# Gated recurrence: the multiplier taken from tanh and a squared, with the order of ScalarE's exponentials, roots and gelus changed

## The reference, cut to what matters

```
def rglru_block(h, w_in, conv_w, conv_b, w_a, b_a, w_x, b_x, lam, w_o):
    proj = h @ w_in
    gate = jax.nn.gelu(proj[..., :RG_WIDTH])
    xc = causal_depthwise_conv_2(proj[..., RG_WIDTH:], conv_w, conv_b)
    ...
    r = jax.nn.sigmoid(... + b_a);  i = jax.nn.sigmoid(... + b_x)
    log_a = (-RG_C * r) * jax.nn.softplus(-lam)
    a = jnp.exp(log_a)
    mult = jnp.sqrt(-jnp.expm1(2.0 * log_a))
    bterm = mult * (i * xc)
    _, hs = lax.associative_scan(lru_combine, (a, bterm), axis=1)
    return (hs * gate) @ w_o
```

## Time and profile before

| what | value |
|---|---|
| median of 3 runs | 1074.45 us (1071.22 to 1075.06) |
| the profiled execution | 1074.95 us, of which the span is 1072.9 us |
| mean granted TensorE clock | 0.992 |
| PE busy | 1022.1 us, 95% of the span |
| DVE busy | 690.9 us, 64% |
| ACT busy | 614.2 us, 57% |

### The profile page before, as it was taken

One profiled execution on the slowest core, in us unless ns is written; L12 is line 12 of the kernel. 1 busy time (PEld: TensorE's weight loads), 2 busy tenths in 40 slices (PEclk: granted clock), 3 DMA queues, 4 the chain that ended last, 5 costly groups with the idle time before them and its releaser, 6 DMA issues. The chain is left out here.

```text
span 1072.9 us, 16887 instructions
## 1 busy us (share of the span) xinstructions
PE 1022.1 (95%) x6978; PEld 923.8 (86%) x6978; DVE 690.9 (64%) x988; ACT 614.2 (57%) x938; POOL 128.4 (12%) x119
## 2 busy tenths in 40 slices
PE   4899999999999999999999899999999989999997
PEld 4899898988998888779888798999889869889995
DVE  5897676857765687776566564545557775555454
ACT  6387677654664656365666654344456975433443
POOL 1010048450200123530000100000000100000000
PEclk9999999999999999999999999999999999999999
DMA  9885245443678432236432465555544354555640
GB/s 334 298 264 156 79 158 197 139 137 92 193 238 273 159 118 80 78 118 210 141 121 79 137 207 179 185 196 183 174 154 158 123 179 169 180 181 189 196 158 39
DMA packets 117499, 178.40 MB, mean 166 GB/s; under 512 B 5204, under 2 KB 74098, under 8 KB 117424
## 3 DMA queue, kind: packets, MB, share of 16 engines
q1 hardware_dynamic: 116160, 174.23, 49.4%
q0 software_dynamic: 1120, 2.97, 0.8%
q10 hardware_dynamic: 144, 0.13, 0.0%
HBM read 176.27 MB, written 1.05 MB: 165 GB/s over the span
## 5 line engine op out<-in xcount | busy, mean ns | idle before, releaser
L1470 DVE TENSOR_TENSOR sb_w_lo<-sb_raw,sb_w_hi 128x2048 fp32r<-128x2048 f32 (+1 forms) x139 | 309.6, 2228 | 201.5 <-ACT sb_w_hi L768 201.2
L768 ACT ACTIVATE sb_w_hi<-sb_raw 128x2048 fp32r<-128x2048 f32 (+1 forms) x135 | 256.3, 1900 | 150.7 <-PE G L2303 116.3
L2301 PE MATMUL X<-sb_hT_hi,sb_w_hi 128*128 128x256 f32 x784 | 223.4, 285 | 5.1 <-DVE sb_hT_lo L1825 3.7
L2302 PE MATMUL X<-sb_hT_lo,sb_w_hi 128*128 128x256 f32 x784 | 221.8, 283 | 0.0
L2303 PE MATMUL X<-sb_hT_hi,sb_w_lo 128*128 128x256 f32 x784 | 221.8, 283 | 0.0
L2301 PEld LDWEIGHTS X<-sb_hT_hi,sb_w_hi 128*128 128x128 f32 x784 | 149.9, 191 | 7.6 <-DVE sb_w_lo L1470 4.3
L2302 PEld LDWEIGHTS X<-sb_hT_lo,sb_w_hi 128*128 128x128 f32 x784 | 150.0, 191 | 0.6
L2303 PEld LDWEIGHTS X<-sb_hT_hi,sb_w_lo 128*128 128x128 f32 x784 | 150.0, 191 | 0.0
L2301 PE MATMUL G<-sb_w_hi,sb_uT_hi 128*128 128x512 f32 x304 | 120.8, 397 | 4.9 <-DVE sb_uT_lo L2241 4.9
L2303 PE MATMUL G<-sb_w_hi,sb_uT_lo 128*128 128x512 f32 x304 | 120.1, 395 | 0.0
L2302 PE MATMUL G<-sb_w_lo,sb_uT_hi 128*128 128x512 f32 x304 | 120.0, 395 | 0.0
(11 more groups left out here) (497 smaller groups left out, 1961.4 us busy)
## 6 DMA issues: line engine op xcount, KB each, us to landing
sb_raw<-in_mlp_w SPq DMA_DIRECT2D x64, 1024.0 KB, 5.2
sb_raw<-in_ada_w SPq DMA_DIRECT2D x24, 1024.0 KB, 5.2
sb_raw<-in_b_in_w SPq DMA_DIRECT2D x16, 1024.0 KB, 5.5
sb_raw<-in_a_in_w SPq DMA_DIRECT2D x14, 1024.0 KB, 5.7
sb_raw<-in_sb_w_qkv SPq DMA_DIRECT2D x12, 1024.0 KB, 5.1
sb_raw<-in_rg_w_in SPq DMA_DIRECT2D x8, 1024.0 KB, 5.4
sb_raw<-in_a_out_w SPq DMA_DIRECT2D x4, 1024.0 KB, 5.1
sb_raw<-in_b_out_w SPq DMA_DIRECT2D x4, 1024.0 KB, 5.1
```

The lines of the kernel that those rows point to most:

```text
L768: nc.scalar.activation(split_tile(w_hi, m)[:, 0:nk * w], raw_of(b)[:, 0:nk * w], ACT.Copy).then_inc(S["w_hi"], 1)
L1470: ins = nc.vector.tensor_tensor(split_tile(w_lo, m)[:, at], raw_of(b)[:, at], split_tile(w_hi, m)[:, at].bitcast(F32), ALU.subtract)
L2301: dt32(out, lh, rh, start=first, stop=False, skip_group_check=shared)
L2302: dt32(out, lh, rl, start=False, stop=False, skip_group_check=shared)
```

## The change

The multiplier becomes the root of t (1 + a²). ScalarE's `rg_logs` makes only the two exponentials; VectorE's `rg_diff` makes a² and then (a² + 1) t; `rg_root` takes the logarithm of that and then exp(0.5 × ...). On ScalarE the exponentials and roots of chunks 2 and 3 move ahead of the first gelus, so that one table change to exponentials goes, and with it one back to gelu. On VectorE `rg_diff` of chunks 2 and 3 moves ahead of `scaled(6)`, and `rg_out` and `rg_lo` of chunks 0 and 1 come behind it.

```
             def rg_logs(c):
                 ch.settle()
-                nc.scalar.activation(den[:, sl2, :], th[:, sl2, :], ACT.Ln, bias=one_col).then_inc(S["rg_logs"], 1)
-                act.wait_ge(S["rg_logs"], 2 * c + 1)
-                nc.scalar.activation(th[:, sl2, :], th[:, sl2, :], ACT.Ln, scale=2.0, bias=const("tiny"))\
-                    .then_inc(S["rg_logs"], 1)
                 for k in (2 * c, 2 * c + 1):
-                    ch.mark(nc.scalar.activation(rr[:, k, :], rr[:, k, :], ACT.Exp, scale=nsl8[:, k:k + 1]))
+                    ins = nc.scalar.activation(rr[:, k, :], rr[:, k, :], ACT.Exp, scale=nsl8[:, k:k + 1])
+                    if k == 2 * c:
+                        ch.mark(ins)
+                ins.then_inc(S["rg_logs"], 1)
...
                 act.wait_ge(S["rg_diff"], c + 1)
-                ch.settle()
+                ch.link(nc.scalar.activation(th[:, sl2, :], th[:, sl2, :], ACT.Ln, bias=const("tiny")))
                 nc.scalar.activation(th[:, sl2, :], th[:, sl2, :], ACT.Exp, scale=0.5).then_inc(S["rg_mult"], 1)
...
             def rg_diff(c):
-                dve.wait_ge(S["rg_logs"], 2 * c + 2)
-                nc.vector.tensor_tensor(th[:, sl2, :], th[:, sl2, :], den[:, sl2, :], ALU.subtract).then_inc(S["rg_diff"], 1)
+                dve.wait_ge(S["rg_logs"], c + 1)
+                ch.link(nc.vector.tensor_tensor(den[:, sl2, :], rr[:, sl2, :], rr[:, sl2, :], ALU.mult))
+                nc.vector.scalar_tensor_tensor(th[:, sl2, :], den[:, sl2, :], 1.0, th[:, sl2, :], ALU.add, ALU.mult)\
+                    .then_inc(S["rg_diff"], 1)
```

More of the change, by code:

```diff
@@ L1410, in _ @@
             rg_logs(0)
+            rg_logs(1)
             rg_block(5)
-            rg_logs(1)
             rg_root(0)
             rg_root(1)
+            rg_logs(2)
+            rg_logs(3)
+            rg_root(2)
+            rg_root(3)
             def rg_gelu(c):
@@ L1431, in _ @@
                 rg_hi(c)
[L1432 to L1436, removed]
             split_for(first_mm["rg_in"] + 7)
@@ L2262, in _ @@
                 rg_scan(c)
+            rg_diff(2)
+            rg_diff(3)
             scaled(6)
@@ L2268, in _ @@
             split_for(first_mm["rg_in"] + 6)
-            rg_diff(2)
             scaled(7)
-            rg_diff(3)
             for c in range(2, 4):
```

## The result

| | median us | ratio to before, 95% interval |
|---|---|---|
| before (10 runs) | 1071.20 | |
| changed (10 runs) | 1076.17 | 1.0039 (1.0028 to 1.0050) |

The change makes the kernel slower by 0.39%, some 4.2 us (the medians alone lie 4.97 apart); 3.2 was forecast. The absolute forecast, 1078.2, is 2 us above the measured 1076.17, and that has a reason of its own, told further down.

What follows compares the result with a forecast made beforehand. TensorE, the fullest engine, was taken to pass lateness at 882 us on one for one. 4.7 us at the turn less 1.5 of clock gave 3.2, on 1074.95 making 1078.2 us; range 1074.8 to 1081.2.

Steps and rivals of the forecast that it cites:

- The chain of chunks 0 and 1: ScalarE and VectorE up to output block 0: ScalarE waits for `rg_diff`, block 0 starts 7.9 us later, TensorE idle 9.6.
- Chunks 2 and 3: VectorE's and TensorE's work up to output block 2: part of the delay comes back, leaving 4.7 us.
- The second gap: TensorE's 3.17 us wait ahead of output block 2, said to close to 0.1 or none.
- Rival 2: VectorE's chain up to chunk 2's output runs 2 us shorter than its times add up to: 1076.2 us; chance 0.13.
- the turn: Start of the next MLP's first block on TensorE, 882.55 before, forecast at 887.3 by the ScalarE and VectorE chain.
- The clock: TensorE's grant in the output blocks: 1.7 us lost behind the stop, at most 2.8, covered if below 2.0.
- the new gap: TensorE's forecast stop of 9.6 us ahead of output block 0.
- rival 1: TensorE's clock costs on the path, from 2.0 us on: +4.7 to +5.7, taken as 1080.6 us; chance 0.22.
- The clock at the turn: Lowered grant from 884.0 to 887.4 lost about 1.5 us before; taken as saved, as TensorE hardly stops there.
- the sum: Whole kernel: 4.7 at the turn less 1.5 of clock gives 3.2 us slower, 1078.2 us; chance 0.55.
- The edits at nothing: ScalarE's two lost table changes (1.28 each) and four logarithms (0.72 each) earn nothing; moved MLP loads are covered.
- rival 3: ScalarE's work on the 838 to 869 us chain is the bound; 5.4 us less gives 1069.5 us; chance 0.06.

Runs made afterwards that it cites:

- gap filled: The changed kernel plus 72 idle matmuls of 256 columns in TensorE's gap ahead of output block 0; ratio to before 1.0057 (1.0037 to 1.0078).
- the reordered kernel: The new arithmetic with one table change each way, VectorE's and ScalarE's queues rearranged to fill waits, against the kernel before; 1067.0 us, ratio 0.9963.

## Why the prediction was right, and where its numbers were off

- **The chain of chunks 0 and 1.** Forecast: output block 0 7.9 later, a gap of 9.6, ScalarE's waits 3.6 and 2.4. Measured: 7.89, 9.56, 3.68 and 2.34. The second instruction of `rg_diff` took 0.69, the lower of its two bounds. Start-to-start times of the old rows, put in the new order, were enough.
- **Chunks 2 and 3.** The second gap was to close to 0.1 or none; it is gone. ScalarE's high part of chunk 2 starts 33.38 behind the table change (868.89 less 835.51) against 28.73 before, 4.65 later; 4.7 was forecast. Rival 2, a chain shorter than its times add up to, did not come: where TensorE's clock is kept full (gap filled), the chain sets the turn at 49.02, and the forecast for it was 49.07 (887.27 less 838.20).
- **The clock.** This is the term that was mis-sized: 1.7 was taken for the lowered grant behind the new gap, with 2.8 as the end of its range. It cost 2.6: the four output blocks take 26.38 (859.02 to 885.40) against 23.74 before (853.82 to 882.55 less the gaps of 3.17 and 1.82). That is beyond the 2.0 at which TensorE itself becomes the last to arrive, as rival 1 put it. The turn is therefore 5.5 late, not 4.7. So it was the path of rival 1, with its chance of 0.22, that set the turn; its price of +4.7 to +5.7 left out the 1.5 that is saved behind the turn, and 5.5 less 1.5 is the 4.0 that came.
- **Where the 1.7 came from.** The row behind it is not a case like the new gap, and was misread: the grant did not fall in the course of that gap but ahead of it, 0.58 over 51 to 52 (so down from about 51.2), while TensorE's transposes ran to 51.6. Part of that lowered stretch passed while TensorE stood; behind the new gap 6.1 us of it fell on matmuls. The 2.8 that the prediction set as the end, all of 6.2 us on matmuls, is 2.7 by its own factor (6.2 x 0.43), and that is what came. The window of before:

```profile
51.00:52.00 1.00, 0.62 (x4) 0.23 (x3) 1.00 (x2) 1.00 (x3) 0.00 (x0) 0.58 1.03 432
```

- **The clock at the turn.** The 1.5 us of lowered grant were to go, and did: 1.00 from 884.0 to 887.4, and the delay shrinks by 1.55 from the turn to the end of the span (5.54 to 3.99). Forecast for the sum 3.2, measured 4.0 in the profiles and 4.2 by the runs. But the two clock terms hang together, which the prediction did not see when it gave the same sum with and without a cost of the new stop. Without that cost TensorE stands at the turn, 2.0 by the prediction's own times, and gap filled shows what follows: a wait of 1.81, a lowered grant, and an end of the span 4.66 later than before (239.36 less 234.70) instead of 3.2.
- **The edits at nothing.** ScalarE's busy time fell by 5.5 us (614.2 to 608.7), as 2 x 1.28 + 4 x 0.72 said, and rival 3, that this work is time, did not come. No load is waited for either: ScalarE's split of the MLP's first block starts 37.84 behind the table change without a wait, and 37.8 (876.0 less 838.20) was forecast. The page's first part of the changed kernel:

```profile
PE 1020.6 (95%) x6978; PEld 922.0 (86%) x6978; DVE 693.5 (65%) x992; ACT 608.7 (57%) x932; POOL 128.3 (12%) x119
```

- **The absolute time.** The sum was set on the profiled execution of before, 1074.95 us, which lies 3.75 above the median of ten runs, 1071.20. The 2.69 us by which it is late at the table change are no work. The first 60 us and the stretch at 260 show more lowered grant than in the changed kernel's profile. Windows of before:

```profile
40.00:60.00 20.00, 17.31 (x128) 16.87 (x127) 15.31 (x21) 8.67 (x10) 0.00 (x0) 0.83 0.71 239
260.00:275.00 15.00, 13.32 (x101) 13.07 (x100) 10.47 (x14) 10.18 (x22) 3.65 (x5) 0.89 0.25 72
```

The same windows of the changed kernel:

```profile
40.00:60.00 20.00, 17.15 (x132) 16.86 (x131) 15.06 (x20) 9.60 (x13) 0.00 (x0) 0.91 0.75 242
260.00:275.00 15.00, 13.30 (x112) 12.86 (x111) 11.87 (x16) 9.80 (x24) 5.46 (x8) 1.00 0.37 103
```

By the grant, before ran 20 x 0.17 = 3.4 us at a loss in the first stretch against 1.8, and 1.7 against 0 in the second; at half speed lost time is about the missing share, so this estimate makes 3.3, of which what fell on TensorE's waits cost nothing. ScalarE's table changes ahead of the recurrence, the same in both kernels, tell where the lead of the changed kernel arose: 0.79 at 65.53, 1.35 at 89.83, still 1.35 at 193.03, 2.60 at 290.13 and 2.69 at 838.20 (times of before). So 1.25 came across the second stretch and 0.79 across the first; 0.56 came between 65 and 90 us, where the grant is full in both, and its cause is open.

The absolute time thus came out near for two errors of opposite sign: the base was 3.75 high, and the difference of the medians was 4.97 where 3.2 was forecast, which leaves 2.0. From the median of ten runs the same sum would have been 1074.4. The 0.5% that the prediction took for the least that can be told from no change was too coarse: ten runs of each tell 0.39% from nothing (1.0028 to 1.0050).

## What to carry to other kernels

Laying the start-to-start times of the old trace along the new queues, engine by engine, gave the waits of a reordered kernel to within 0.1 us; here the order within each queue decided, not the sum of its work. Work batched by function table has a place in the queue: put ahead of what TensorE waited for, it cost 0.39%, and with both queues arranged around it the kernel gained 0.37%. Count from the last instruction that a change leaves alone: the seven profiles here, of kernels that agree up to it, reach it between 835.01 and 838.43 us. And ask of a lowered clock what waits behind it, as a stop that is filled in one place may open in the next.

## What the runs showed of the hardware that was not expected

- A gap of 1.81 to 1.82 us at the turn was followed by 3.2 to 3.4 us of lowered grant in two profiles (before, and gap filled), while a gap of 3.17 us in the kernel before was not the earlier trace rows. In the new arithmetic with the old order it was the other way round: the grant fell behind the recorded gap of 2.65 ahead of output block 0 and stayed full behind the same 1.81 at the turn. The length of a gap alone did not tell whether the grant fell. Windows of before, around the gap of 3.17:

```profile
866.00:868.00 2.00, 0.00 (x0) 0.00 (x0) 1.90 (x4) 1.07 (x2) 0.00 (x0) 1.00 0.20 56
868.00:870.00 2.00, 1.57 (x7) 1.34 (x8) 0.89 (x3) 1.98 (x3) 0.00 (x0) 1.00 0.95 317
```

TensorE's timeline of the new arithmetic with the old order at the turn:

```profile
882.55 0.36 PE L2302 MATMUL X<-sb_hT_hi,sb_w_hi 128*128 128x256 f32 x1 [1.81 <-DVE sb_hT_lo L1824]
```

Its windows, behind the two gaps:

```profile
856.00:858.00 2.00, 2.00 (x6) 1.61 (x5) 1.97 (x3) 1.06 (x3) 0.00 (x0) 0.50 0.00 0
...
884.00:886.00 2.00, 2.00 (x19) 2.00 (x19) 0.37 (x1) 0.00 (x0) 0.00 (x0) 1.00 0.94 385
```

- Keeping TensorE busy with idle matmuls held the grant at 1.00 through a stretch of 9.4 us and the blocks behind it, and saved 2.7 us there, but no time of the kernel.
- The lowered stretches far from the change differ from profile to profile: 420 to 440 us reads 1.00 in before and in the changed kernel; in the reordered kernel its window reads 0.83:

```profile
420.00:440.00 20.00, 18.34 (x105) 15.86 (x103) 16.43 (x51) 13.06 (x35) 10.45 (x8) 0.83 0.32 106
```
